# The delta rule's VectorE order: where the block inverse is joined in even steps, and its four-wide joining in odd steps

## The reference, cut to what matters

```python
decay = jnp.exp(jnp.where(tri, gcum[..., :, None] - gcum[..., None, :], -jnp.inf))
kk = jnp.einsum('bhid,bhjd->bhij', kc, kc)
m = jnp.where(strict, bc[..., :, None] * kk * decay, 0.0)
sol = lax.linalg.triangular_solve(eye + m, rhs, left_side=True, lower=True, unit_diagonal=True)
v_new = u - jnp.einsum('bhid,bhdv->bhiv', w, s)
```

## Time and profile before

| what | value |
|---|---|
| median of 3 runs | 2783.94 us (2782.05 to 2784.24) |
| the profiled execution's own time | 2783.11 us |
| its span in the profile | 2781.3 us |
| mean granted TensorE clock | 0.987 |
| busy: PE / DVE / ACT / POOL | 96% / 64% / 24% / 39% of the span |
| delta pipeline, steps -1 to 15 | from 1394.5 to 1712.7 us |

### The profile page before, as it was taken

The page is one execution under the profiler, slowest core; times in us unless marked ns, Lnnn a source line. Parts: engine busy times, 40 slices in busy tenths (PEclk is TensorE's granted clock), DMA queues, the critical chain, the costliest instruction groups (busy, mean ns, idle before and its releaser), DMA issues.

```text
span 2781.3 us, 42210 instructions
## 1 busy us (share of the span) xinstructions
PE 2675.1 (96%) x16211; PEld 2288.8 (82%) x16211; DVE 1787.6 (64%) x3138; ACT 668.8 (24%) x1404; POOL 1089.6 (39%) x809
## 2 busy tenths in 40 slices
PE   6999999999999999999889899999999999999998
PEld 4865888888786999887478888888888886798998
DVE  4557778777555797688657765875456873334862
ACT  2124222210224220254346554211000002322000
POOL 3411245555320566232244433553454440021665
PEclk9999999999999999999989999999999999999999
DMA  7236222247527545322223323222224653112443
GB/s 280 76 114 265 109 97 91 91 152 272 182 90 289 197 168 182 150 78 84 60 75 73 89 57 97 76 88 79 90 78 148 223 204 126 61 46 76 152 167 122
DMA packets 113696, 358.42 MB, mean 129 GB/s; under 512 B 41792, under 2 KB 60992, under 8 KB 79072
## 3 DMA queue, kind: packets, MB, share of 16 engines
q1 hardware_dynamic: 81248, 296.90, 30.2%
q10 hardware_dynamic: 30672, 53.68, 5.7%
q0 software_dynamic: 1584, 5.21, 0.6%
HBM read 345.15 MB, written 10.62 MB: 128 GB/s over the span
## 4 chain that ended last, share of the span: by engine, by line
PE 87%; DVE 6%; ACT 4%; DMA 2%; issue 1%; DVEq 1%; SPq 0%; POOLq 0%; POOL 0%; ACTq 0%
PE psum L3507 49%; PE psum L251 7%; PE psum L1837 5%; PE psum L3500 2%; PE psum L3013 2%; PE psum L276 2%; PE psum L766 1%; DMA ring<-in_stream 1%; PE psum L2062 1%; PE psum L582 1%; PE psum L425 1%; PE psum L2044 1%; PE psum L3131 1%; PE psum L595 1%; PE psum L613 1%
## 5 line engine op out<-in xcount | busy, mean ns | idle before, releaser
L3507 PE MATMUL psum<-arena,ring 128*128 128x256 f32 (+1 forms) x3336 | 606.1, 334 | 0.2 <-DVE arena L3595 0.2
L3507 PEld LDWEIGHTS psum<-arena,ring 128*128 128x128 f32 x3336 | 528.3, 191 | 50.1 <-DVE arena L3595 0.6
L3507 PE MATMUL psum<-arena,c 128*128 128x256 f32 (+1 forms) x2088 | 390.4, 336 | 0.0
L3507 PEld LDWEIGHTS psum<-arena,c 128*128 128x128 f32 x2088 | 334.6, 191 | 33.3 <-issue 1.9
L3537 POOL TENSOR_TENSOR c<-ring 128x512 f32<-128x512 f32 (+1 forms) x81 | 106.2, 1311 | 639.5 <-PE psum L3507 319.9
L3539 POOL TENSOR_TENSOR ring<-ring 128x512 f32<-128x512 f32 x169 | 263.7, 1560 | 36.9 <-issue 13.3
L3553 ACT COPY kst<-psum 128x256 f32<-128x256 f32 (+1 forms) x114 | 37.5, 329 | 908.3 <-PE psum L3507 723.5
L3507 PE MATMUL psum<-h_sb,ring 128*128 128x256 f32 (+1 forms) x1376 | 252.9, 337 | 2.2 <-DVE kst L3613 2.2
L3541 POOL TENSOR_TENSOR c<-ring 128x512 f32<-128x512 f32 x158 | 234.3, 1483 | 22.5
L3507 PEld LDWEIGHTS psum<-h_sb,ring 128*128 128x128 f32 x1376 | 220.3, 192 | 25.6 <-issue 4.6
L3537 POOL TENSOR_TENSOR rows<-ring 128x512 f32<-128x512 f32 (+1 forms) x70 | 92.2, 1317 | 294.9 <-PE psum L3507 262.1
(11 more groups left out here) (450 smaller groups left out, 5018.0 us busy)
## 6 DMA issues: line engine op xcount, KB each, us to landing
ring<-in_stream SPq DMA_DIRECT2D x266, 1024.0 KB, 4.9
arena<-in_ada_rows ACTq DMA_DIRECT2D x32, 512.0 KB, 5.2
h_sb<-in_late ACTq DMA_DIRECT2D x24, 512.0 KB, 4.8
arena<-decays SPq DMA_DIRECT2D x24, 256.0 KB, 4.9
silu_w<-in_late ACTq DMA_DIRECT2D x12, 512.0 KB, 4.5
ring<-gsums SPq DMA_DIRECT2D x20, 256.0 KB, 4.2
keys_d<-kst ACTq DMA_DIRECT2D x16, 256.0 KB, 3.4
arena<-gsums SPq DMA_DIRECT2D x12, 256.0 KB, 4.1
```

What stands on the lines that cost most here:

```text
L3507: ins = pe.matmul(dst, self.seven_weights(n, i, k, nk, w_sums), self.seven_moving(x, sums, i, k, nk, width), start=first and j == 0 and k ...
```

## The change

In even steps the pair side 1 of size 8 and `dve_inverse_out` goes from in front of the level-4 right sum to behind the level-5 mask. In odd steps (from 1 on), the first pass (side 0) of size 4 goes from behind the level-5 right sum to in front of it; the second pass stays behind. No instruction is added or removed, and no other engine's order is touched.

```diff
-            if last is not None:
-                self.dve_inverse_side(dve, last, 8, (0,), 1)
-                self.dve_inverse_out(dve, last)
             if a is not None:
                 self.dve_right(dve, a, 4)
             if n is not None:
                 self.dve_keys(dve, n, 0)
             if a is not None:
                 self.dve_left(dve, a, 5)
+            if last is not None:
+                self.dve_inverse_side(dve, last, 8, (0,), 1)
+                self.dve_inverse_out(dve, last)
             if m is not None and s > 0:
                 self.dve_inverse_fours(dve, m)
+            if m is not None and s > 0:
+                self.dve_inverse_side(dve, m, 4, (0, 8 * (BASE + 1)), 0)
             if a is not None:
                 self.dve_right(dve, a, 5)
             if m is not None and s > 0:
-                self.dve_inverse_eights(dve, m)
+                self.dve_inverse_side(dve, m, 4, (0, 8 * (BASE + 1)), 1)
```

## The result

| what | before | after |
|---|---|---|
| median | 2783.94 us (5 runs) | 2807.67 us (5 runs, 2805.20 to 2810.70) |
| ratio | | 1.0093, interval 1.0081 to 1.0104 |
| the profiled execution / its span | 2783.11 / 2781.3 us | 2805.20 / 2803.4 us |
| mean granted TensorE clock | 0.987 | 0.983 |
| first level-4 product to the end of the delta pipeline | 318.3 us | 343.2 us |

The changed kernel is 0.9% slower. The forecast was slower too, but by 15 us, and this is 24 by the medians and 26 by the ratio. 2807.67 lies 1.3 us inside the range given; the ratio on the median of before gives 2809.8, just outside it. The pipeline alone grew by 24.9 us. (What lies outside it took 2.8 us less in this profile.) One execution of a later kernel, e8, took 10813.13 us at a mean clock of 0.567 and is left out of its median.

The account below looks back on a forecast made before the run. TensorE was busy 96%, but a serial path through SyncE's gate sums was nearly critical in odd steps. 16.1 + 0.9 + 2.7 - 4.4 = +15.3 us gave 2799 us, range 2787 to 2809 (own case 2794 to 2806).

Parts of the forecast that it names:

- The bound and the path: Odd steps: serial path VectorE copy, SyncE, DRAM, gate sums, GpSimd, ScalarE, TensorE, only 1.04 us short of the critical one.
- faster: Rival: the DRAM trip isn't on the chain, so the gains stand alone, 7.2 us, 2776.7; chance 0.09.
- nothing: Rival: gains and losses are both hidden by TensorE's 96%, 2784 us; chance 0.05.
- only `id`: Rival: gate sums in time but the inverse's blocks late, +3.7 us, 2787.6; chance 0.07.
- two signs of being wrong: Either no new ScalarE idle in front of L2439, or the granted clock below 1.00 in odd steps.
- Part A: Even steps: inverse's last pass and copy behind the level-5 mask; signal `inv` comes mask start plus 2.83 us, 4.0 to 7.5 later.
- Steps 2, 6 and 10: Even steps where TensorE's 0.94 us wait in front of the level-5 left product was to go.
- the gate sums': Odd steps 1 to 9: gate sums leave SyncE 17.1 us later in sum, of which 16.1 falls on the chain.
- The clock: Rival: TensorE's clock falls in the new odd-step waits, 1 to 3 us in up to five steps, 2801 to 2813; chance 0.17.
- Step 11: No gate sums loaded; wait for `id` at the level-4 product, +0.9 us, bounds 0 and 4.0.
- part B: Odd steps: size-4 side 0 ahead of the level-5 right sum; 0.88 us gained in steps 1 to 9, 4.4 in all, 0 in step 11.
- Step 13: No gate sums loaded; GpSimd's spread of the inverse's blocks delays the level-4 product, +2.7 us, upper bound 5.1.

Follow-up runs that it names:

- e8: Kernel before, with the odd steps' move, and the inverse's last pass and copy directly behind the level-4 right sum in steps 2, 6, 10: 2777.92 us.
- e4: Changed kernel, with the inverse's second load on its own semaphore, issued straight behind the first: 2790.61 us, ratio 1.0035.
- e6: Kernel before, with the even steps' move in steps 10 and 12 only: 2787.61 us, ratio 1.0018.
- e14: Changed kernel run again unaltered, as comparison for a kernel with filled waits: 2803.93 us, ratio 1.0093.
- e12: Changed kernel, with the gate sums of odd steps held until the inverse's second load has landed: 2817.83 us in one run.
- e9: Changed kernel run again unaltered, in another batch: 2800.50 us, ratio 1.0082.
- e1: Kernel before, with the even steps' move alone: 2809.72 us, ratio 1.0094.
- e5: Changed kernel, with the gate sums of odd steps issued one step early by ScalarE's queue instead of SyncE's: 2806.36 us, ratio 1.0083.
- e2: Kernel before, with the odd steps' move alone: 2779.66 us, ratio 0.9981.
- e11: Kernel before, odd steps' move, inverse's last pass and copy behind the level-4 right sum in steps 2, 6, 10, its two loads issued together: 2773.85 us.
- e15: Kernel before, odd steps' move, inverse's last pass and copy behind the level-4 right sum in all even steps, its loads issued together: 2774.64 us.
- e3: Changed kernel, with ten unread products each ahead of the level-5 queries and level-5 turn in steps 1, 3, 5, 7, 9: 2808.89 us.

## Why the prediction was right and wrong

**The bound and the path: right.** Where the gate sums leave, what they delay, and where TensorE then waits came out in each place named: SyncE's issue straight behind the second load, ScalarE's idle for L2548 (2.45 to 3.16 us, forecast 1.5 to 4), the 0.94 at L2044 gone, the longest wait for L2569 in step 13 (2.33). e4 shows that the path is the cause of most of it. The rivals "faster" and "nothing" fell, and so did "only `id`": e6 gives `id` alone 5.0 us, not the whole. One of the text's two signs of being wrong did show, though: in steps 5 and 9 of the first profile the granted clock fell below 1.00.

**Part A's signal: right in time, a little off in effect.** The signal came 2.86 us behind the mask (2.83). Steps 2, 6 and 10 gained 0.55 us each, not 0.94. TensorE's idle in front of the left product is gone, but 0.33 us of a new one stands in front of the level-5 right product in step 2 of after, released by ScalarE's L2487, whose queue has no gap from decays 0 (L2439) on: the next one in line, which the prediction hadn't named.

**The mis-sized term is the gate sums'**: +16.1 forecast, +18.8 where the clock stayed up. The step that failed is the one that kept the old durations for transfers in a new order. When the gate sums leave was right: counted as the forecast counts, 16.9 us later over the five steps in e14, forecast 17.1, although they follow the second load by 0.49 to 0.51 us where the forecast had 0.39. What failed is the landing. The forecast took 5.8 us from issue to bars, and they took 5.9 to 7.0 in e14, 3.1 us more over the five than before. With the 0.2 less at the issue and 0.2 more absorbed on the way, 2.7 reached the end. The text named 0.5 us in five landings as its largest uncertainty, in both directions; but only one direction was open. Before, the inverse's second load had 1.4 to 2.8 us to itself; now the gate sums always follow it at once. e12 and the durations of the other profiles show that this is what slows them. (The bounds as listed add up to 2792.7 to 2806.8; the text gave 2794 to 2806 for its own case.)

**The clock: too small a chance.** It had 0.17 and an argument from one row, that the clock stayed at 1.00 through 10 us with TensorE busy for 6.76. The first profile has four falls, the one in step 4 behind a wait of 1.86 us. That a stretch once kept its clock is no proof that it will: in e14 it did, with the same waits, and in the first profile it didn't. The price per fall, 0.9 us and more, was about what the rival said (1 to 3), and its range, 2801 to 2813, holds two of the three medians; e9's lies 0.5 under it. The rule of the Trainium skill named there (page "TensorE: Matmul & The Clock Gate", section "HAM oscillation — how this bites in real kernels") would have made this rival the likelier one, and the first profile agrees with it. Those of e9 and e14 don't, since the waits were there and the falls were not. The page tells its rule of a kernel whose waits are longer than the 0.4 to 1.9 us of these odd steps.

**Small terms.** Step 11 lost 1.8 to 2.2, not 0.9, within its bounds of 0 and 4. e6, without the gate sums, lost 1.1 there, and e1, with them and without part B, 1.0. What is more comes from part B, which the forecast set at 0 in this step. VectorE of before in step 11, then GpSimd and VectorE of e14:

```profile
1645.81 0.69 DVE L2805 TENSOR_TENSOR rows<-psum,c 128x512 f32<-128x512 f32 x1 [2.10 <-PE psum L2044]
...
1649.03 0.69 DVE L2813 TENSOR_TENSOR ring<-ring,psum 128x512 f32<-128x512 f32 x1 [1.20 <-PE psum L2062]
```
```profile
1657.11 2.26 POOL L2569 TENSOR_TENSOR ring<-gates,small 128x512 f32<-128x512 f32 x2
1658.56 0.83 DVE L2852 TENSOR_TENSOR blk<-vec 128x8 f32<-128x8 f32 x1
1661.12 0.69 DVE L2815 TENSOR_TENSOR ring<-ring,psum 128x512 f32<-128x512 f32 x1
```

From the level-5 mask to the right sum it is 3.22 us before, 1.20 of them idle. In e14, where the mask starts at 1657.18, it is 3.94, with no idle time left: the moved pass takes 0.88, and two operations ahead of it, under GpSimd's late spread, take 0.9 longer (0.66 and 0.83 us; before, with GpSimd idle, 0.41 and 0.17). In the first profile it is 4.33. In every profile without part B, or with it but with the spread over before those two operations, it is 3.22 or 3.23. So here the cover was gone, and the pass made the right sum late by 0.7 to 1.1 us. Step 13 lost 2.6 without and 4.1 with a fall (2.7). Steps 0 and 12, set at nothing, cost 0.3 each or more. In steps 1 to 9 part B gave 5.4, not 4.4.

**Together**: with the terms as measured the sum is 19.9 in e14's profile and 24.9, with four falls of the clock more, in the first. 15.3 was too low in each profile. The range, which ended at 2809, held the medians of all three batches, the first by 1.3 us; but the ratios to the kernel before in the same batch, 1.0093, 1.0082 and 1.0093, stand for 2809.8, 2806.8 and 2809.8 on its median, two of them just outside. So its end was too low as well.

Two things stay open: why the clock falls in one execution and not in another with the same waits, and whether it can be bought back by filling them.

## What to carry to other kernels

Before moving a step on one engine, find out whose queue waits for its signal and what stands behind that wait. Here an order on VectorE, at 64%, cost 20 us and more through loads on SyncE that had nothing to do with it and only 1 to 2.4 us of slack. When a change makes transfers follow each other without a gap, don't price them with durations from when they had one; add to the range on that side alone. And when a change adds waits of 1 to 2 us to a loop of matmuls, run it more than once before explaining a few us: the clock may fall in one execution and not in the next. A free place in front of a wait is free only as long as the operations ahead of it keep their durations.

## What the runs showed of the hardware

- Transfers in flight together slow one another. Two gate sum rows of 256 KB each are at the bars 5.05 to 5.81 us after their issue when the 64 KB load ahead of them has landed (e12), and 5.9 to 7.0 when it is in flight (e14). The first 64 KB load of a batch takes 2.3 to 2.7 us in after and 4.6 to 6.2 with the rows in flight (e5).
- The granted clock fell to 0.50 behind a wait of 1.86 us in one execution and stayed at 1.00 behind one of 1.84 us at the same place in another. Over 17 runs of the changed kernel a mean clock of 0.987 or more goes with 2800.5 us on average, 0.983 or less with 2808.9.
- Two small VectorE operations of 0.41 and 0.17 us took 0.66 and 0.83 while GpSimd worked (e14, step 11; before, e2, e4, e8, e11 and e15, with GpSimd idle, 0.41 or 0.42 and 0.17).
- A float32 product of 128 columns is two instructions, about 0.24 us together: ten products, twenty instructions, took 2.39 us (e3).
